# The opening of a two-block transformer kernel, put in another order

## The reference

```
def rms_norm(x, g):
    y = xf * lax.rsqrt(jnp.mean(xf * xf, axis=-1, keepdims=True) + EPS)
    return (y * g.astype(jnp.float32)).astype(x.dtype)

def ada_mod(c, w, b, n):
    h = jax.nn.silu(c) @ w + b
    return jnp.split(h[:, None, :], n, axis=-1)

def gmlp_layer(x, c, ada_w, ada_b, norm_g, w_in, sgu_g, w_s, b_s, w_out):
    shift, scale, gate = ada_mod(c, ada_w, ada_b, 3)
    h = rms_norm(x, norm_g) * (1 + scale) + shift
    u, v, z = jnp.split(h @ w_in, 3, axis=-1)
    ...
```

## Time and profile before

| what | us |
|---|---|
| runs | 1417.32, 1414.81, 1417.15 |
| median of runs | 1417.15 |
| profiled execution, time | 1414.09 |
| profiled execution, span | 1412.1 |
| TensorE busy | 1392.8 (99%) |
| VectorE busy | 990.3 (70%) |
| ScalarE busy | 648.1 (46%) |

### The profile page before, as it was taken

One profiled execution on the slowest core, in us unless ns is written; L12 is line 12 of the kernel. 1 busy time (PEld: TensorE's weight loads), 2 busy tenths in 40 slices (PEclk: granted clock), 3 DMA queues, 4 the chain that ended last, 5 costly groups with the idle time before them and its releaser, 6 DMA issues.

```text
span 1412.1 us, 19654 instructions
## 1 busy us (share of the span) xinstructions
PE 1392.8 (99%) x7278; PEld 1157.7 (82%) x7278; DVE 990.3 (70%) x1530; ACT 648.1 (46%) x1046; POOL 50.9 (4%) x55
## 2 busy tenths in 40 slices
PE   8999999999999999999999999999999999999999
PEld 6998888888888888888887777776688888888887
DVE  6976777777898788888877788989775343332333
ACT  5744222233366566666644666666543322211221
POOL 0001000001100000000002000000030000000000
PEclk9999999999999999999999999999999999999999
DMA  9994444457723211121113221121132223222222
GB/s 377 380 377 181 179 178 178 178 220 285 277 90 105 90 61 61 60 82 67 60 60 120 81 83 61 47 73 49 37 113 90 89 89 108 100 90 96 99 80 82
DMA packets 35328, 181.22 MB, mean 128 GB/s; under 512 B 4153, under 2 KB 4921, under 8 KB 20930
## 3 DMA queue, kind: packets, MB, share of 16 engines
q1 hardware_dynamic: 34050, 177.95, 34.1%
q10 hardware_dynamic: 1216, 2.44, 0.6%
HBM read 177.74 MB, written 2.11 MB: 127 GB/s over the span
## 4 chain that ended last, share of the span: by engine, by line
PE 83%; DVE 10%; DMA 3%; ACT 2%; issue 2%; SPq 0%; DVEq 0%; ACTq 0%
PE acc L1748 73%; PE ada L1748 3%; DMA ada_out<-in_ada 3%; PE norm L1748 2%; DVE w_lo L1007 2%; PE turn L1748 2%; DVE s L999 1%; DVE stat L1585 1%; PE turn L2041 1%; PE turn L2180 1%; DVE qk L999 1%; DVE hx L999 1%; DVE hk_lo L999 0%; DVE y_half L999 0%; DVE ada_out L999 0%
## 5 line engine op out<-in xcount | busy, mean ns | idle before, releaser
L1748 PE MATMUL acc<-h_hi,w_hi 128*128 128x512 f32 x984 | 389.7, 396 | 0.1
L1748 PE MATMUL acc<-h_hi,w_lo 128*128 128x512 f32 x984 | 383.9, 390 | 0.0
L1748 PE MATMUL acc<-h_lo,w_hi 128*128 128x512 f32 x984 | 383.3, 390 | 0.0
L1007 DVE TENSOR_TENSOR w_lo<-w_raw,w_hi 128x2048 fp32r<-128x2048 f32 (+1 forms) x96 | 222.0, 2312 | 58.7 <-ACT w_hi L574 58.7
L574 ACT ACTIVATE w_hi<-w_raw 128x2048 fp32r<-128x2048 f32 (+1 forms) x96 | 181.7, 1893 | 116.5 <-PE acc L1748 116.4
L1748 PEld LDWEIGHTS acc<-h_hi,w_lo 128*128 128x128 f32 x984 | 184.7, 188 | 39.7
L1748 PEld LDWEIGHTS acc<-h_hi,w_hi 128*128 128x128 f32 x984 | 185.0, 188 | 38.8 <-issue 1.8
L1748 PEld LDWEIGHTS acc<-h_lo,w_hi 128*128 128x128 f32 x984 | 185.0, 188 | 37.1 <-issue 0.2
L999 DVE SCALAR_TENSOR_TENSOR x<-acc,mods,x 128x512 f32<-128x512 f32 (+1 forms) x40 | 33.0, 828 | 82.2 <-PE acc L1748 82.2
L1748 PE MATMUL acc<-wv_hi,h_hi 128*128 128x256 f32 x320 | 89.7, 281 | 0.6 <-DVE wv_lo L1007 0.6
L1748 PE MATMUL acc<-wv_lo,h_hi 128*128 128x256 f32 x320 | 88.3, 277 | 0.0
(11 more groups left out here) (305 smaller groups left out, 2535.4 us busy)
## 6 DMA issues: line engine op xcount, KB each, us to landing
w_raw<-in_weights SPq DMA_DIRECT2D x102, 1024.0 KB, 4.8
ada_v<-in_ada SPq DMA_DIRECT2D x32, 512.0 KB, 6.4
ada_raw<-in_ada SPq DMA_DIRECT2D x32, 512.0 KB, 5.6
ada_out<-in_ada SPq DMA_DIRECT2D x32, 512.0 KB, 6.3
ada_up<-in_ada_first SPq DMA_DIRECT2D x8, 1024.0 KB, 16.8
w_raw<-in_weights SPq DMA_DIRECT2D x4, 768.0 KB, 4.0
x<-in_x SPq DMA_DIRECT2D x2, 1024.0 KB, 6.1
w_first<-in_weights SPq DMA_DIRECT2D x4, 512.0 KB, 13.4
```

The lines of the kernel that those rows point to most:

```text
L1007: nc.vector.tensor_tensor(lo[:, 0:used], w_raw[par][:, 0:used], f32(hi[:, 0:used]), ALU.subtract).then_inc(lo_done, 1)
L1748: return nc.tensor.matmul(out, lhsT, rhs, start=start, stop=stop)
```

## The change

On GpSimd, idle is cleared first. TensorE multiplies eleven times by zeros before c is spread, and none behind it. ScalarE squares tiles 0, 1, 2, 4, 5, 6 of x, and then does the two Silu. VectorE squares tiles 3 and 7 itself and adds in the same pairs. up_unit keeps only the two products; VectorE makes gains_a = (1 + bias of scale) * g for all eight tiles once, and ScalarE makes the gain as scale * g + gains_a and adds the bias to shift, both ahead of h_full in its loop. The first tile of x_n is scaled by y0 and finished with the Newton factor; x_rstd and the other tiles follow. The six small gains move behind the mask of ws_t. Counts of sq_ready and the index of hx_start are adapted. gains_a takes the place of row_weight.

```diff
@@ gpsimd
+            nc.gpsimd.memset(idle[:, :].bitcast(F32), 0.0).then_inc(idle_ready, 1)
             nc.gpsimd.memset(one_row[:, :], 1.0).then_inc(one_ready, 1)
-            nc.gpsimd.memset(idle[:, :].bitcast(F32), 0.0).then_inc(idle_ready, 1)
@@ scalar
+            for kt in (0, 1, 2, 4, 5, 6):
+                act.wait_ge(x_loaded[kt // 4], 16)
+                nc.scalar.activation(sq_first[kt][:, :], x[:, kt, :], ACT.Square).then_inc(sq_ready, 1)
             for n in range(2):
                 act.wait_ge(c_spread_in, n + 1)
                 nc.scalar.activation(csil[0][:, TOK * n:TOK * n + TOK], G[n][:, :], ACT.Silu).then_inc(csil_ready, 1)
-            for kt in range(KT):
-                act.wait_ge(x_loaded[kt // 4], 16)
-                nc.scalar.activation(sq_first[kt][:, :], x[:, kt, :], ACT.Square).then_inc(sq_ready, 1)
             act.preload_act_table_set("natural_log_exp_and_others")
             rstd_start(N_X0, NB[:, :], DM, True)
+            act.wait_ge(g_ready, 1)
             for kt in range(KT):
                 if kt == KT - 1:
                     to_hi(1, 0)
+                shift, scale = [mods[:, 2 * kt + e:2 * kt + e + 1] for e in range(2)]
+                gain = gscale[:, kt:kt + 1]
+                act.wait_ge(up_done, 2 * kt + 2)
+                nc.scalar.activation(gain, scale, ACT.Identity, bias=gains_a[:, kt:kt + 1], scale=vecs[:, G_A + kt:G_A + kt + 1]).then_inc(gsa_done, 1)
+                nc.scalar.activation(shift, shift, ACT.Identity, bias=mod_bias[:, 2 * kt:2 * kt + 1]).then_inc(gsa_done, 1)
                 act.wait_ge(xn_done, kt + 1)
-                act.wait_ge(gsa_done, kt + 1)
-                shift, gain = mods[:, SHIFT_A + 2 * kt:SHIFT_A + 2 * kt + 1], gscale[:, kt:kt + 1]
+                act.wait_ge(gsa_done, 2 * kt + 2)
                 nc.scalar.activation(h_full[:, kt, :], x_n[:, kt, :], ACT.Identity, bias=shift, scale=gain).then_inc(hx_done, 1)
@@ vector, up_unit
-                dve.wait_ge(up_done, 2 * kt + 2)
-                pair = slice(2 * kt, 2 * kt + 2)
-                nc.vector.tensor_tensor(mods[:, pair], mods[:, pair], mod_bias[:, pair], ALU.add).then_inc(up_out, 1)
-                dve.wait_ge(up_out, kt + 1)
-                stt(gscale[:, kt:kt + 1], mods[:, SCALE_A + 2 * kt:SCALE_A + 2 * kt + 1], 1.0, vecs[:, G_A + kt:G_A + kt + 1],
-                    ALU.add, ALU.mult).then_inc(gsa_done, 1)
@@ vector
-            for i in range(KT // 2):
-                dve.wait_ge(sq_ready, 2 * i + 2)
-                nc.vector.tensor_tensor(sq_first[2 * i][:, :], sq_first[2 * i][:, :], sq_first[2 * i + 1][:, :], ALU.add)\
-                    .then_inc(sq_added, 1 + i // 2)
+            for half in range(2):
+                dve.wait_ge(x_loaded[half], 16)
+                last = sq_first[4 * half + 3][:, :]
+                nc.vector.tensor_tensor(last, x[:, 4 * half + 3, :], x[:, 4 * half + 3, :], ALU.mult).then_inc(sq_vector, 1)
+                for kt in (4 * half, 4 * half + 2):
+                    dve.wait_ge(sq_ready, 3 * half + (2 if kt % 4 == 0 else 3))
+                    if kt % 4:
+                        dve.wait_ge(sq_vector, half + 1)
+                    nc.vector.tensor_tensor(sq_first[kt][:, :], sq_first[kt][:, :], sq_first[kt + 1][:, :], ALU.add).then_inc(sq_added, 1 + half)
             dve.wait_ge(vecs_loaded, 16)
-            (the six operations that make gains)
+            scales = mod_bias[:, 0:FIRST_MODS].rearrange("p (k e) -> p e k", e=2)[:, 1, :]
+            stt(gains_a[:, :], scales, 1.0, vecs[:, G_A:G_A + 8], ALU.add, ALU.mult).then_inc(g_ready, 1)
             dve.wait_ge(csil_ready, 2)
             up_unit(0)
-            rstd_end(N_X0, NB[:, :], DM, x_rstd)
-            for kt in range(KT):
+            dve.wait_ge(y0_done, 1)
+            nc.vector.tensor_tensor(x_n[:, 0, :], x[:, 0, :], y0[:, :], ALU.mult).then_inc(hx_start, 1)
+            dve.wait_ge(half_done, 1)
+            stt(y0_half[:, :], NB[:, :], DM * EPS, y0_half[:, :], ALU.add, ALU.mult).then_inc(newton_done, 1)
+            dve.wait_ge(newton_done, 1)
+            dve.wait_ge(hx_start, 1)
+            stt(x_n[:, 0, :], y0_half[:, :], 1.5, x_n[:, 0, :], ALU.subtract, ALU.mult, reverse0=True).then_inc(xn_done, 1)
+            stt(x_rstd[:, :], y0_half[:, :], 1.5, y0[:, :], ALU.subtract, ALU.mult, reverse0=True).then_inc(rstd_done, 1)
+            dve.wait_ge(rstd_done, 1)
+            for kt in range(1, KT):
                 nc.vector.tensor_tensor(x_n[:, kt, :], x[:, kt, :], x_rstd[:, :], ALU.mult).then_inc(xn_done, 1)
-                if kt > 0:
-                    up_unit(kt)
+                up_unit(kt)
@@ vector, behind the mask of ws_t
+            (the six operations that make gains)
@@ tensor
+            pe.wait_ge(idle_ready, 1)
+            stay_busy(11)
             pe.wait_ge(one_ready, 1)
             pe.wait_ge(c_loaded, 16)
             for n in range(2):
                 mm(G[n][:, :], one_row[:, :], c_in[:, TOK * n:TOK * n + TOK], True, True).then_inc(c_spread_in, 1)
-            pe.wait_ge(idle_ready, 1)
-            stay_busy(6)
```

More of the change, by code:

```diff
@@ L162, in program @@
     row_max, row_sum, row_inv, row_weight = [at(f"row_{name}", [P, 8], take(32, 32)) for name in ("max", "sum", "inv", "weight")]
+    gains_a = row_weight
     lam_inv = at("lam_inv", [P, 2], take(8, 32))
@@ L289, in program @@
     ada_done, mods_ready = sem("ada_done"), sem("mods_ready")
-    up_done, up_out, gsa_done = sem("up_done"), sem("up_out"), sem("gsa_done")
+    up_done, g_ready, gsa_done = sem("up_done"), sem("g_ready"), sem("gsa_done")
     xn_done, one_ready, idle_ready = sem("xn_done"), sem("one_ready"), sem("idle_ready")
@@ L295, in program @@
     lam_part, lam_exp, lam_ready = sem("lam_part"), sem("lam_exp"), sem("lam_ready")
-    sq_ready, sq_added, qsq_ready = sem("sq_ready"), sem("sq_added"), sem("qsq_ready")
+    sq_vector, sq_ready, sq_added, qsq_ready = sem("sq_vector"), sem("sq_ready"), sem("sq_added"), sem("qsq_ready")
     qlo_ready, half_zeroed, half_ready = sem("qlo_ready"), sem("half_zeroed"), sem("half_ready")
@@ L520, in sum_squares @@
                 for m in range(1, KT - 1):
-                    pool.wait_ge(sq_ready, 8 * k + m + 1)
+                    pool.wait_ge(sq_ready, 8 * k - 2 + m + 1)
                     if m > 1:
@@ L1042, in gain @@
                 dve.wait_ge(gs_done, e)
[L1044 to L1050, removed]
             def square_rest(n, hi, full, lo):
@@ L1164, in _ @@
-            for i in range(KT // 2):
-                dve.wait_ge(sq_ready, 2 * i + 2)
-                nc.vector.tensor_tensor(sq_first[2 * i][:, :], sq_first[2 * i][:, :], sq_first[2 * i + 1][:, :], ALU.add)\
-                    .then_inc(sq_added, 1 + i // 2)
-            dve.wait_ge(vecs_loaded, 16)
-            nc.vector.tensor_scalar(gains[:, 0:1], vecs[:, G_QB:G_QB + 1], P ** -0.5, None, ALU.mult)
-            nc.vector.tensor_scalar(gains[:, 1:2], vecs[:, G_FQ:G_FQ + 1], 0.125, None, ALU.mult)
@@ L1171, in _ @@
-            nc.vector.tensor_copy(gains[:, 2:3], vecs[:, G_FK:G_FK + 1])
-            nc.vector.tensor_scalar(gains[:, 3:4], vecs[:, G_DQ:G_DQ + 1], 0.125, None, ALU.mult)
-            nc.vector.tensor_copy(gains[:, 4:5], vecs[:, G_DK:G_DK + 1])
-            nc.vector.tensor_scalar(gains[:, 5:6], vecs[:, G_DN:G_DN + 1], 1.0 - LAM_INIT, None, ALU.mult).then_inc(gains_ready, 1)
+            for half in range(2):
[7 more added lines that the diff above has]
+                    nc.vector.tensor_tensor(sq_first[kt][:, :], sq_first[kt][:, :], sq_first[kt + 1][:, :], ALU.add).then_inc(sq_added, 1 + half)
@@ L1194, in _ @@
             nc.vector.tensor_tensor(ws_t[:, :, :], ws_t[:, :, :], tri, ALU.mult).then_inc(ws_ready, 1)
+            nc.vector.tensor_scalar(gains[:, 0:1], vecs[:, G_QB:G_QB + 1], P ** -0.5, None, ALU.mult)
+            nc.vector.tensor_scalar(gains[:, 1:2], vecs[:, G_FQ:G_FQ + 1], 0.125, None, ALU.mult)
+            nc.vector.tensor_copy(gains[:, 2:3], vecs[:, G_FK:G_FK + 1])
+            nc.vector.tensor_scalar(gains[:, 3:4], vecs[:, G_DQ:G_DQ + 1], 0.125, None, ALU.mult)
+            nc.vector.tensor_copy(gains[:, 4:5], vecs[:, G_DK:G_DK + 1])
+            nc.vector.tensor_scalar(gains[:, 5:6], vecs[:, G_DN:G_DN + 1], 1.0 - LAM_INIT, None, ALU.mult).then_inc(gains_ready, 1)
             dve.wait_ge(small_loaded, 64)
@@ L1263, in _ @@
             x_rest(0, KT - 1, True)
-            x_norm(N_X1, 1, 0)
+            x_norm(N_X1, 1, 1)
             h_split(1, SHIFT_KV, True, (hk_hi, hk_lo))
@@ L1519, in _ @@
             x_rest(1, KT - 1)
-            x_norm(N_X2, 3, 1)
+            x_norm(N_X2, 3, 2)
             nc.vector.memset(gate_one[:, :], 1.0).then_inc(fgate_dve, 1)
@@ L1691, in _ @@
             x_rest(2, KT - 1)
-            x_norm(N_X3, 4, 2)
+            x_norm(N_X3, 4, 3)
             h_split(4, SHIFT_2, False)
@@ L1792, in add_squares @@
                 mm(NB[:, :], ones, sq_sum[:, :], True, False)
```

(2 more changed lines are left out.)

## The result

| | before | after |
|---|---|---|
| median of 22 runs each, same chip | 1417.34 (1413.09 to 1420.58) | 1419.6 (1416.75 to 1421.77) |
| mean of these runs | 1416.98 | 1419.47 |
| ratio, 95% interval | | 1.0019 [1.0011, 1.0026] |
| profiled execution, span / time | 1412.1 / 1414.09 | 1416.7 / 1418.71 |
| TensorE busy | 1392.8 | 1397.1 |

The kernel became slower: by 2.3 us between the medians and 2.5 between the means, where 0.3 faster was forecast. The ratio is just inside the 0.2% that were called no change, but its interval leaves out 1. The runs of one kernel spread over some 7.5 us, so only the many runs show it.

What follows compares the result with a forecast made beforehand. TensorE bounds the kernel; only its opening waits count. A 2.0 us earlier first tile shrinks to 0.95 at the second and 0.3 at k = 3's load: 1417.15 becomes 1416.8, range 1416.5 to 1417.1 (0.1 to 0.6 gained, chance 0.52).

Steps and rivals of the forecast that it cites:

- ScalarE ahead of the logarithm: Opening: two Silu behind the squares, then one 1.28 us table load, so the logarithm starts at 12.7, 1.3 us gained.
- If the clock again rises 5.7 us after they begin: TensorE's zeros ahead of the spread: begun at about 1.35, they raise the clock at 7.1; the spread ends at 8.3.
- The cover: Wait between ScalarE's table load and the logarithm in the kernel before: 1.67 us; the logarithm was to come 1.3 sooner.
- That load already sets its pace: VectorE in the kernel before: it starts on k = 3 at 25.25, at once when the modulation rows land.
- The last addition on VectorE: Squares shared by ScalarE and VectorE: last addition of squares runs 10.6 to 11.3, 0.5 us earlier than before.
- The first h_full: First tile from the first estimate: starts 3.5 us behind the logarithm, at 16.2 instead of 18.20; TensorE at 17.1.
- The second tile: Its x_n waits for x_rstd: TensorE starts it at 21.6 after a 1.0 us wait, cutting the 2.0 gain to 0.95.
- The load of k = 3: Modulation rows land at 25.2; VectorE waits about 1.5 us, TensorE 0.6, leaving 0.3 us gained.
- The slow one: Rival in spread and sums: zeros fail to raise TensorE's clock, sums end at 16.4, 2.6 us slower, 1419.8; chance 0.13.
- The longer ScalarE: Rival at the table load: it needs the old waiting time, logarithm at 14.4, end 0.5 us later, 1417.6; chance 0.05.
- The full opening: Rival: k = 3's modulation rows land a microsecond sooner, the second tile limits, 0.95 us gained, 1416.2; chance 0.2.
- Something given back later: Rival behind the opening: the 0.3 us disappears in a later wait for weights or loads, 1417.1; chance 0.1.

Runs made afterwards that it cites:

- a_table: The changed kernel with ScalarE's first table load naming silu_and_others, the set holding Square and Silu: median 1416.4 us, ratio 1.0005 to the kernel before.
- t_table: The changed kernel with its first table load naming silu_and_others, cut off behind the v phase: 120.47 to 123.67 us.
- a_full2: The changed kernel whole, unaltered, timed again with more runs: median 1419.52 us of 5, ratio 1.0017 to the kernel before.
- t_zeros: The kernel before with only the zeros moved ahead of the spread (eleven, idle cleared first), cut behind the v phase: mean 127.22 us.
- t_load: Cut changed kernel with silu_and_others loaded first and k = 3's modulation rows loaded ahead of w_first's second half: mean 123.20 us.
- best17: Whole changed kernel with silu_and_others first, k = 3's rows ahead of w_first's second half, 17 zeros ahead of the spread: 1417.67 us, ratio 1.0004 to before.
- a_again: The changed kernel once more, unaltered, for a second profile: 1421.7 us, one run.
- a_fill11: The changed kernel with 11 instead of 16 zeros behind the row sums: median 1418.89 us, ratio 1.0012 to the kernel before.
- t_after: The changed kernel cut off behind the v phase, all later work left out: 121.70 to 124.38 us.
- t_after2: The changed kernel cut off behind the v phase, repeated for more single executions: 121.67 to 125.72 us.
- t_before: The kernel before cut off behind the v phase, all later work left out: 120.66 to 123.36 us.
- t_before2: The kernel before cut off behind the v phase, repeated for more single executions: 120.24 to 123.39 us.
- b_fill21: The kernel before with 21 instead of 16 zeros behind the row sums: median 1418.11 us, ratio 1.0015 to the kernel before.
- combo: Whole changed kernel with spread, zeros and Silu in their old order and k = 3's rows loaded ahead of w_first's second half: 1416.51 us, ratio 1.0000 to before.
- t_best17: Cut changed kernel with silu_and_others first, k = 3's rows ahead of w_first's second half, 17 zeros ahead of the spread: 120.61 to 125.28 us.

## Why the prediction was wrong

**Two steps failed.**

*"ScalarE ahead of the logarithm."* The sum had Silu directly behind the squares and one load behind it: 10.35 to 11.4, 12.7. In after, with Square as the first function, the load at 0.74 didn't serve Silu, which had its own: 1.28 us at 10.52, and the logarithm came at 14.21. Putting Silu's set first (a_table, t_table) brought the table back to 12.64 and took 0.8 us off the cut kernel within a cluster. This step sets the logarithm in every profile of after but one. The traces show one load between Square and Silu in after, none in a_table, and none between Silu and Square in before. The prediction took the price of a load from the earlier trace rows, 1.28, and did not count the loads.

*"If the clock again rises 5.7 us after they begin."* One execution was taken for a rule. In ten of the profiles of kernels with the zeros ahead the clock rose at 4.7 to 7.3, and in five of those ten it fell again between 8.1 and 10.8, to a granted clock of 0.50. The sums wait for their squares in four of these five, but they do so too in four of the five in which it didn't fall, so that wait is not shown to be the cause; in a_full2 it rose at 14.4 and in t_zeros at 17.4. In those with the spread first it rose between 8.9 and 12.1, and didn't fall: the granted clock reads 1.00 in them up to 19 us. There all of TensorE's full-height work, zeros, sums and more zeros, stands in one piece; the change cuts it in two with the one-row spread between. In a_full2 and t_zeros the spread did nothing for the clock, as in before: its last two loads still take 0.33, at 7.32 and 8.18 in a_full2, at 7.34 and 8.19 in t_zeros, at 3.46 and 4.32 in before.

The two prices can be told apart by the logarithm. With neither fault it came at 12.7 to 13.1 (t_table, t_load, best17), with the fallen clock alone at 13.59 (a_table), with the load alone at 13.98 and 14.05 (a_again, a_fill11), with both at 14.1 to 14.5 (after, t_after, t_after2), where only the load counts, and with the load and a late clock at 15.90 (a_full2). So the load is the common price, 0.8 to 1.0 us within a cluster of the cut kernels, and the late clock adds 1.8 us in the one execution of after in which it was profiled; over all of them the cut kernel lost 1.08.

**The cover was read off one execution as well.** The 1.67 of waiting ahead of the logarithm counted as time to be won from TensorE. With the clock at 8.9, as in t_before and t_before2, 0.71 of it is left, and their openings end 0.5 to 0.7 sooner than the profile said; b_fill21 has 1.78. So in some executions the change had less to win than 1.3, even if both steps had held.

**A reading of rows that doesn't hold.** "That load already sets its pace" was said of k = 3 in before. VectorE's unit of k = 2 starts 3.28 us ahead of that of k = 3 (25.25), and the next one 3.28 behind it, at 28.53, with no wait for a load between 15 and 48 us:

```profile
21.97 1.22 DVE L999 SCALAR_TENSOR_TENSOR ada_up<-ada_up,csil 128x1024 f32<-128x1024 f32 x1
```

In that execution VectorE ran at its own pace and the load landed just in time. In t_before and t_before2, which begin the product sooner, VectorE does wait for it, 0.7 and 0.5 us, as the sum has it for after.

**The steps that held.** The last addition on VectorE ended at 10.08 + 1.29 = 11.37 (11.3 forecast). The first h_full came 3.5 behind the logarithm, at 17.71, and TensorE 0.9 later (18.62). The second tile started 8.65 behind the logarithm (8.6), with a wait of 0.55 ahead of it (1.0 forecast). From the end of the unit of k = 3 to its h_full it took 28.74 - 28.05 = 0.69 (0.7 forecast). The load of k = 3 landed at 25.7 (25.2) and VectorE waited for it:

```profile
25.66 1.23 DVE L1005 SCALAR_TENSOR_TENSOR ada_up<-ada_up,csil 128x1024 f32<-128x1024 f32 x1 [0.87 <-DMA ada_up<-in_ada_first]
```

The forecast was 1.5 there; with the logarithm 1.5 late, VectorE came later too, and this load was no longer the limit: the second tile was. In t_load, where it is issued earlier, the end followed the second tile alone, as the sum had it.

**The rivals.** The slow one came true in at least one execution of after: a_full2 kept the low level through the spread and up to 14.4, with loads of 0.33 to 0.34, and lost 2.0 of its 2.6 us. That the one-row spread holds the clock down is not shown by it. It decides where it was put, once the sums end after 13.8. Its chance was given for the whole kernel, though it is drawn anew in each execution, and the milder form, a clock that rises and falls again, wasn't thought of. The longer ScalarE was wrong: the time that came was a second load, and behind each load the next activation starts within 0.02 us (10.52 + 1.28, 11.81; 12.91 + 1.28, 14.21). The full opening didn't come: the logarithm was late, and the load of k = 3 landed at 25.7 and not sooner. Something given back later is not ruled out, but not in the v phase: in before and in after the 576 matmuls there follow each other without a gap behind the first.

**What stays open.** The means of the full kernels differ by 2.5 us (a_full2: 1419.35 against 1416.92, 2.4), the opening explains 1.1. Some 1.3 us are not settled. Between the profiled pair the rest lies in two places behind the opening: 2.5 us in the v phase's pitch, which is a toss per execution, and 1.6 us between the first matmul on y_hi and the second row sum of the norm near 395 us (91.29 before, 92.87 after), where VectorE waits for ada_out:

```profile
DVE ada_out L1005 <- DMA ada_out<-in_ada: 18.7, 7, 4.9
```

against 17.1 in eight waits before. But that stage took 91.03 in a_fill11 and 92.78 in a_table, so it scatters by as much as the two differ. From there to the last matmul it is 1016.0 and 1016.15. The pitch could favour before only if its odds differ: the four profiled full executions of after and a_fill11 all had the longer one and the two of before and b_fill21 the shorter, but best17 had the longer and a_table and combo the shorter, and of the cut kernels half of before's 14 and some four of after's 11 times lie in the upper cluster or above it. The runs can't tell more.

One part of the scatter of the full runs can be read. In some executions the clock falls far behind the opening, while TensorE is busy. combo, from 395 to 412 us (us, PE busy (x), PEclk, DMA share, GB/s):

```profile
395.00:412.00 17.00, 17.00 (x106) 0.90 0.19 63
```

The same stretch of before reads 1.00. Combo's clock falls once more near 1060 us (0.92 from 1060 to 1080), and from that second row sum to the last matmul it takes 1017.5, 1.5 more than before. a_fill11, a_table and best17, with as much time at the low level (0.91 in each of 400 to 420 and 1060 to 1080; 0.91 and 0.93; 0.83 in the first alone), take 1017.3 to 1017.6; a_again, with two and a half times as much (0.91 from 400 to 420, 0.83 from 980 to 1000 and from 1060 to 1080), takes 1020.2; before, b_fill21, after and a_full2, with none, take 1016.0 to 1016.2. The executions of before show it too: on the chip of a_table those with a mean granted clock of 1.00 have spans of 1411.1 to 1413.8, those with 0.994 of 1418.2 and 1418.7. So this is no property of the change, but it and the pitch make up much of the 7 to 8 us.

## What to carry to other kernels

Before moving a function on ScalarE, count the table loads of the new order, and look in the trace for those between two functions: here Silu ahead of Square had none between them (before), and Square ahead of Silu had one of 1.28 us (after), until silu_and_others was named first (a_table). Work that is there to raise TensorE's clock is worth what it does in every execution (with the zeros ahead it rose at 4.7 to 7.3 in ten profiles, at 14.4 and 17.4 in two), so read the time of the rise in several profiles, and keep that work in one piece with what needs the clock: in the eight profiles that had it so, the clock didn't fall again in the opening. A stall that one profile shows is one draw (0.71 to 1.78 us in the kernels that keep before's opening), and so not what can be won on average, and a cut kernel of a tenth of the length shows a microsecond that the full one hides in its scatter.

## What the runs showed of the hardware

The pitch of the v phase's matmuls has two values. Two stretches of the timeline, first before, then after:

```profile
69.97 0.28 PE L1748 MATMUL acc<-wv_hi,h_hi 128*128 128x256 f32 x1
...
70.64 0.28 PE L1748 MATMUL acc<-wv_hi,h_hi 128*128 128x256 f32 x1
```

```profile
69.76 0.28 PE L1753 MATMUL acc<-wv_hi,h_hi 128*128 128x256 f32 x1
...
70.46 0.28 PE L1753 MATMUL acc<-wv_hi,h_hi 128*128 128x256 f32 x1
```

Six matmuls on, 0.67 against 0.70 us; behind the first few matmuls it is 113.3 or 117.8 ns each. An execution takes one of the two within the first six matmuls and keeps it to the end of the phase: 65.48 or 68.03 us for 576. The granted clock reads 1.00 in both from 47 to 114 us, and the instructions of the phase are the same. In the cut kernels the profiled executions tie it to the clusters: with 113.3 t_after took 121.99, t_after2 121.67 and t_table 120.47; with 117.8 t_before took 123.36 and t_before2 123.19. Both clusters stand in the times of one program, so it seems to do either, but no program was profiled at both. t_best17's 123.04 had 113.3 and a logarithm 2.4 us late, so a time alone doesn't tell the two apart. What decides the pitch is open: not the place of the instructions in the program (b_fill21, a_fill11), and not when the clock rose (8.9 with the longer in t_before, 11.9 with the shorter in before, 14.4 with the longer in a_full2).
